# A two-layer decoder trunk on one core: 32x32 transposes on VectorE and DMAs between partition groups in place of TensorE transposes

## What is computed

```python
# layer one: stick-breaking attention
q, k, v, z = split(x @ w_in_a)                 # 2048 -> 4 x 2048
w = exp(log_sigmoid(s) + tail(log_sigmoid(-s)))  # s = q k^T / sqrt(128), past keys
y = ((w @ v) * silu(z)) @ w_out_a
# after each layer
x = layer_norm(2**0.5 * x + y)
x = x + (p[i] @ w_ple[i]) * sigmoid(x @ w_ple_gate[i])
# layer two: causal softmax attention against a shared, rotary K/V
k, v = split(layer_norm_kv(x) @ w_kv); k = rope(k)
q, z = split(x @ w_in_b);              q = rope(q)
y = ((softmax(q k^T / sqrt(128)) @ v) * silu(z)) @ w_out_b
```

## Time and profile before

| | |
|---|---|
| median of three runs | 1171.24 us |
| the profiled execution's own time | 1170.72 us |
| its span, first to last instruction | 1168.8 us |
| TensorE busy | 1161.9 us, 99% |
| VectorE busy | 740.9 us, 63% |
| ScalarE busy | 591.1 us, 51% |
| share of the 16 DMA engines, queue of SyncE | 57.7% |

### The profile page before, as it was taken

One profiled execution on the slowest core, in us unless ns is written; L12 is line 12 of the kernel. 1 busy time (PEld: TensorE's weight loads), 2 busy tenths in 40 slices (PEclk: granted clock), 3 DMA queues, 4 the chain that ended last, 5 costly groups with the idle time before them and its releaser, 6 DMA issues.

```text
span 1168.8 us, 15615 instructions
## 1 busy us (share of the span) xinstructions
PE 1161.9 (99%) x5484; PEld 971.4 (83%) x5484; DVE 740.9 (63%) x786; ACT 591.1 (51%) x669; POOL 21.3 (2%) x43
## 2 busy tenths in 40 slices
PE   9999999999999999999999999999999999999998
PEld 7888888888888888888888888888888888888886
DVE  6765556556556556688777665446677666656863
ACT  6665465456446543455444445544555545435541
POOL 1000000000000000000000000000000000000000
PEclk9999999999999999999999999999999999999999
DMA  9855656665565776457765655655545575763671
GB/s 307 287 161 178 181 162 178 179 181 161 165 194 156 241 253 200 137 184 237 232 198 162 197 180 182 193 181 164 169 155 178 167 244 175 252 195 112 211 252 41
DMA packets 112618, 221.49 MB, mean 189 GB/s; under 512 B 6929, under 2 KB 8977, under 8 KB 112065
## 3 DMA queue, kind: packets, MB, share of 16 engines
q1 hardware_dynamic: 110032, 209.74, 57.7%
q0 software_dynamic: 2544, 11.19, 2.7%
HBM read 216.71 MB, written 4.19 MB: 189 GB/s over the span
## 4 chain that ended last, share of the span: by engine, by line
PE 95%; DVE 2%; DMA 1%; ACT 1%; issue 0%; SPq 0%; ACTq 0%; DVEq 0%
PE acc L1077 29%; PE acc L1079 29%; PE acc L1078 29%; PE aux L1104 2%; PE aux L1121 2%; DVE w_lo L676 1%; PE aux L1145 1%; DVE stage L870 1%; PE aux L1159 1%; DMA raw<-in_w_ple_gate 1%; PE aux L1308 0%; DMA raw<-in_w_in_a 0%; DVE act L691 0%; PE aux L1079 0%; PE aux L1078 0%
## 5 line engine op out<-in xcount | busy, mean ns | idle before, releaser
L676 DVE TENSOR_TENSOR w_lo<-raw,w_hi 128x1024 fp32r<-128x1024 f32 x388 | 471.7, 1224 | 358.5 <-ACT w_hi L417 357.2
L417 ACT ACTIVATE w_hi<-raw 128x1024 fp32r<-128x1024 f32 x388 | 409.7, 1060 | 471.3 <-PE acc L1079 424.5
L1077 PE MATMUL acc<-w_hi,act 128*128 128x512 f32 x1552 | 611.9, 394 | 0.2 <-DVE w_lo L767 0.2
L1079 PE MATMUL acc<-w_hi,act 128*128 128x512 f32 x1552 | 605.1, 390 | 0.0
L1078 PE MATMUL acc<-w_lo,act 128*128 128x512 f32 x1552 | 604.1, 389 | 0.0
L1079 PEld LDWEIGHTS acc<-w_hi,act 128*128 128x128 f32 x1552 | 291.3, 188 | 61.8
L1077 PEld LDWEIGHTS acc<-w_hi,act 128*128 128x128 f32 x1552 | 291.5, 188 | 58.6 <-issue 1.0
L1078 PEld LDWEIGHTS acc<-w_lo,act 128*128 128x128 f32 x1552 | 291.7, 188 | 58.1
L430 ACT ACTIVATE act<-stage 128x1024 fp32r<-128x1024 f32 (+1 forms) x12 | 12.7, 1061 | 33.8 <-DVE stage L870 33.8
L513 ACT ACTIVATE heads<-aux,neg_max 128x128 f32<-128x128 f32 (+1 forms) x32 | 13.0, 419 | 23.7 <-DVE neg_max L1000 23.7
L691 DVE TENSOR_TENSOR act<-stage,act 128x1024 fp32r<-128x1024 f32 (+1 forms) x12 | 14.7, 1226 | 14.3 <-ACT act L430 14.3
(11 more groups left out here) (148 smaller groups left out, 617.5 us busy)
## 6 DMA issues: line engine op xcount, KB each, us to landing
raw<-in_w_in_a SPq DMA_DIRECT2D x124, 512.0 KB, 3.7
raw<-in_w_ple_gate SPq DMA_DIRECT2D x64, 512.0 KB, 4.8
raw<-in_w_in_b SPq DMA_DIRECT2D x64, 512.0 KB, 3.7
raw<-in_w_kv SPq DMA_DIRECT2D x64, 512.0 KB, 3.7
raw<-in_w_out_a SPq DMA_DIRECT2D x32, 512.0 KB, 4.4
raw<-in_w_out_b SPq DMA_DIRECT2D x32, 512.0 KB, 4.9
heads<-in_ln_rows POOLq DMA_DIRECT2D x4, 1024.0 KB, 8.2
raw<-in_w_ple SPq DMA_DIRECT2D x8, 512.0 KB, 4.6
```

Of the source, the lines that this page charges most:

```text
L417: nc.scalar.activation(w_hi[:, r], raw[:, r % RAWS], ACT.Copy).then_inc(hi_ready, 1)
L676: nc.vector.tensor_tensor(w_lo[:, r], raw[:, r % RAWS], w_hi[:, r].bitcast(F32), ALU.subtract) \
L1077: nc.tensor.matmul(dst, hi, w_hi[:, r, i], start=begin, stop=False)
L1079: mm = nc.tensor.matmul(dst, lo, w_hi[:, r, i], start=False, stop=end)
```

## The change

All transposes of q, k and z in layer one, of q and z in layer two, of the key/value operand and of three of four quarters of x2 leave TensorE. In their place:

- VectorE transposes 32x32 blocks (`turn_squares`, `turn_queries`, `turn_normed`, a step in `add_ple`), 128x1024 in one instruction. For q, k, z it takes the place of the copy out of `acc`.
- SyncE then moves the blocks between groups of 32 partitions: `exchange` issues 16 DMAs of 32 partitions x 256 values (32 KB each), in four batches of four, each batch after one of its loads. The batches stand after loads 3, 4, 5, 6 of a chunk (SOON), or eight after load 5 and eight after load 6 (LATE), or after 1 and 2 (MIDDLE).
- ScalarE and VectorE read the blocks through access patterns that put them in order, from SBUF instead of PSUM (`q_copies`, `k_copies`, `silu_z`, `x2_hi`, `ln_quarter`); `q_copies` copies all 256 tokens twice.
- The steps on the other engines move: `x2_hi` from after piece 3 to 6, `copy_qT` from 2 to 6, `silu_z` of layer two from 2 to 5. `k_copies` stays after piece 2 and `key_scores` after piece 4.
- The copy of x2 after its sum is gone.
- The last ple product of layer two (12 matmuls of 128x512) goes behind the last gate chunk, as 18 matmuls in three parts (`last_ple_product`), and the final product, sum and store are cut into three parts.

```diff
@@ SyncE @@
+            def exchange(turned, count, dst, src, moved, at):
+
+                def group(i):
+                    if i == 0:
+                        sp.wait_ge(turned, count)
+                    rows = slice(i * SQUARE, (i + 1) * SQUARE)
+                    for g in range(NS):
+                        sp.dma_start(dst[g * SQUARE:(g + 1) * SQUARE, i * HT // NS:(i + 1) * HT // NS],
+                                     src[rows, g * HT // NS:(g + 1) * HT // NS]).then_inc(moved, 16)
+
+                return {j: [lambda i=i: group(i) for i in range(NS) if at[i] == j] for j in at}
+
+            SOON, LATE, MIDDLE = (3, 4, 5, 6), (5, 5, 6, 6), (1, 1, 2, 2)
...
-                load_chunk(n, 0, wa, g + 2 * G)
-                load_chunk(n + PC, 0, wa, g + 3 * G)
+                load_chunk(n, 0, wa, g + 2 * G, q_exchange_a(g * 4))
+                load_chunk(n + PC, 0, wa, g + 3 * G, k_exchange_a(g * 4 + 1))
                 load_chunk(n + 2 * PC, 0, wa, g + 1)
-                load_chunk(n + 3 * PC, 0, wa, g + 1 + G)
+                load_chunk(n + 3 * PC, 0, wa, g + 1 + G, z_exchange_a(g * 4 + 3))
...
+            with sp.Fori(2, G + 2) as c:
+                load_chunk(c * PC + N_Q, N_Q, wb, c, ln_exchange(c - 2) | q_exchange(c - 2))
@@ ScalarE @@
             def k_copies(k):
 
-                act.wait_ge(kT_psum, k + 1)
-                nc.scalar.activation(kT[:, :, P:T], aux_kt[1][:, :, P:T], ACT.Copy).then_inc(kT_ready, 1)
-                nc.scalar.activation(k_parts[:, 0], aux_kt[1][:, :, 0:P], ACT.Copy).then_inc(k_hi, 1)
+                act.wait_ge(k_moved, k * MOVED + MOVED)
+                nc.scalar.activation(by_square(k_own), kT_x[:, 1::TT], ACT.Copy).then_inc(kT_ready, 1)
+                nc.scalar.activation(by_square(k_parts[:, 0]), kT_x[:, 0::TT], ACT.Copy).then_inc(k_hi, 1)
@@ VectorE @@
-            def evacuate(n_end, parity, dst):
+            def turn_squares(n_end, parity, dst):
+
                 dve.wait_ge(piece_used, n_end)
-                nc.vector.tensor_scalar(dst, acc_of(parity), 1.0, None, ALU.mult).then_inc(chunk_evac, 1)
+                nc.vector.transpose(turned_squares(dst), turned_rows(acc_of(parity))).then_inc(chunk_evac, 1)
...
+                nc.vector.tensor_tensor(r, r, stage_tn, ALU.add).then_inc(x2_ready, 1)
+                if layer == 0:
+                    dve.wait_ge(x2_ready, e + 1)
+                    if turn:
+                        nc.vector.transpose(turned_squares(vz_flat), turned_rows(r)).then_inc(x2_turned, 1)
+                    statistics(r, c)
@@ TensorE @@
             def after_v(k, c):
-                return {2: [lambda: k_turn(k, c - 1)], 4: [lambda: key_scores(k, 0)],
+                return {4: [lambda: key_scores(k, 0)],
                         5: [lambda: key_scores(k, 1)]}
...
-            with pe.Fori(1, G) as c:
-                chunk(c * PC + N_Q, N_Q, act1, c % 2, c + C_Q,
-                      after={2: [lambda: q_turn_b(c - 1)], 5: [lambda: ln_step(c)]})
-            chunk(N_Z, N_Z, act1, 0, C_Z, after={2: [lambda: q_turn_b(G - 1)]})
-            with pe.Fori(1, G) as c:
-                chunk(c * PC + N_Z, N_Z, act1, c % 2, c + C_Z, after={2: [lambda: z_turn_b(c - 1)]})
+            chunk(N_Q, N_Q, act1, 0, C_Q, quarters=S_X2, after={2: [last_x2_turn]})
+            with pe.Fori(1, 2 * G) as c:
+                chunk(c * PC + N_Q, N_Q, act1, c % 2, c + C_Q)
```

More of the change, by code:

```diff
@@ L926, in out_ple_gate @@
                           + [lambda r=r: normalise(r, r) for r in x1] + turned[0]})
-                pieces(N_PLE[layer], N_PLE[layer], count=G,
-                       before={0: turned[1], 2: turned[2]})
+                pieces(N_PLE[layer], N_PLE[layer], count=G - layer,
+                       before={0: turned[1], 2 - layer: turned[2]})
                 n = N_GATE[layer]
-                pieces(n, n, {4: [lambda: gain_and_offset(layer, 0)], PC - 1: [lambda: add_ple(layer, 0)]},
+                pieces(n, n, {4: [lambda: gain_and_offset(layer, 0)], PC - 1: [lambda: add_ple(layer, 0, layer == 0)]},
@@ L931, in out_ple_gate @@
                        before={0: turned[3]})
-                with dve.Fori(1, G - layer) as c:
-                    pieces(c * PC + n, n, ({3: [lambda: x2_lo(c - 1)]} if layer == 0 else {})
-                           | {5: [lambda: gain_and_offset(layer, c)], PC - 1: [lambda: add_ple(layer, c)]})
+                if layer == 0:
+                    for c in range(1, G):
+                        pieces(c * PC + n, n, {5: [lambda: gain_and_offset(0, c)], 6: [lambda: x2_lo(c - 1)],
+                                               PC - 1: [lambda: add_ple(0, c, c < G - 1)]})
+                else:
+                    with dve.Fori(1, G - 1) as c:
+                        pieces(c * PC + n, n, {5: [lambda: gain_and_offset(1, c)], PC - 1: [lambda: add_ple(1, c)]})
@@ L935, in out_ple_gate @@
                 if layer:
                     c = G - 1
+                    pieces(n + c * PC, n, count=1)
                     gain_and_offset(layer, c)
-                    dve.wait_ge(ple_evac, 2 * G)
                     dve.wait_ge(x1_ready, 2 * G)
-                    for t in range(TT):
-                        r, gate = columns(res[1], c)[:, t], stage_tn[:, t]
+                    for i, (t, lo, hi) in enumerate(LAST_PARTS):
+                        r, gate = columns(res[1], c)[:, t, lo:hi], stage_tn[:, t, lo:hi]
@@ L990, in k_end @@
+            pieces(N_Z, N_Z, {2: [lambda: ln_quarter(G - 1)], 3: [lambda: ln_lo(G - 1)]} | z_end(0, 0))
+            for c in range(1, G):
+                pieces(c * PC + N_Z, N_Z, z_end(c, c % 2))
             def k_end(n, g):
@@ L1194, in _ @@
             chunk(0, 0, act0, 0, 0, quarters=S_X)
-            chunk(PC, 0, act0, 1, 1, after=after_k(0, 1))
+            chunk(PC, 0, act0, 1, 1)
             pe.wait_ge(masks_done, 1)
@@ L1236, in ple_and_gate @@
                 pe.wait_ge(p_ready, layer + 1)
-                for c in range(G):
+                for c in range(G - layer):
                     n = N_PLE[layer] + c
@@ L1248, in ple_and_gate @@
                 chunk(n, n, act0, 0, c0, quarters=s, after={1: [lambda: turn(3)]})
[L1249 removed]
+                if layer == 0:
+                    pe.wait_ge(ple_evac, G)
                 with pe.Fori(1, G - layer) as c:
[L1251 to L1252 removed]
+                    chunk(c * PC + n, n, act0, c % 2, c + c0)
                 if layer:
```

338 lines of the change are left out of this document (198 added, 140 removed).

## The result

The changed kernel takes 1231.41 us, the median of four runs (1228.64 to 1232.58), against 1171.07 us for the kernel before on the same chip: a ratio of 1.0513, 95% interval 1.0494 to 1.0531. It is 5.1% slower. I had forecast 1166.5 us, a range of 1152 to 1175, and a chance of 0.14 for slower. Both sign and size were wrong. The profiled execution took 1228.64 us, its span is 1226.7 us.

The account below looks back on a forecast made before the run. TensorE, busy 99% of the span, was taken as the bound. From 1170.72 us: -23.9 transposes, +9.9 and +7.5 waits before the scores, +2.0 clock, +0.8 norm, -0.5 end = 1166.5 us, range 1152 to 1175.

Parts of the forecast that it names:

- the waits before the scores: Layer one, TensorE waiting for k: +7.5 us in the first head group and 3 x 3.3 = +9.9 us in the others.
- the low clock: TensorE's clock falls once, behind the 7.5 us wait, and stays low 4 us: +2.0 us, bounds 0 and 4.
- the norm: Layer two, gate product one ple piece earlier against the norm, so its operand comes late: +0.8 us, bounds 0 and 2.
- The end: After the last matmul: sigmoid and most products lie beside the last ple product, two half-width instructions follow: -0.5 us.
- step 2: SyncE issues k's four batches 0.47 us per DMA; load 6 waits for v's lo part, last DMA out at 161.05.
- Behind the wait nothing starves: Layer one, groups two to four: weight parts run eight pieces (21.8 us) ahead, so TensorE does not lack weights.
- the tightest place: SyncE in layer two's q chunks: 40 issues at 0.47 take 18.8 of 21.8 us; exchanges there cost nothing in the sum.
- 0 to 2 us is in the range: The x2 exchange makes the sigmoid up to 5 us later; x2's last transposes have about half a microsecond left.
- the row at the end: Profile row after the last matmul: clock falls some 4.8 us after TensorE stopped, so waits of 3.3 us were thought too short.
- Late landing: Rival: 32 KB DMAs of the k exchanges and first q exchange land 4.2 us after issue: 1183 us, chance 0.14.
- nothing much: Rival: small waits (first group 10, clock 4, x2 2) eat the advance: 1171 us, chance 0.14.
- the low bounds of the steps: Layer one, the path to k at its lowest step times: 1.3 us of wait a group said to remain.

Follow-up runs that it names:

- experiment 1: The changed kernel with each exchange as 4 DMAs of 128 partitions instead of 16, same bytes, movement between partition groups left out, result not valid: 1176.58 us.
- experiment 7: The changed kernel with 8 of the 16 DMAs of every exchange issued by GpSimd and 8 by SyncE: 1156.72 us, ratio 0.9876 to the kernel before.
- experiment 12: The kernel of experiment 7 unchanged, measured once more on the same chip: 1156.31 us, ratio 0.9865 to the kernel before.

## Why the prediction was wrong

Against the profiled execution, 1228.64 us, the forecast of 1166.5 lacks 62.1 us. By its terms: the waits before the scores were 41.3 us where the sum had 17.4 (23.9 too little); x2, the last z, the out projection and the weight parts waited 25.3 us, for which it had nothing; the low clock cost 15.5 us for 2.0; the norm cost nothing for 0.8.

**What held.** 104 of 320 transposes are left; with the account above, 0.887 us for a group of eight is right. The block transpose took 1.24 us for the 1.22 taken. The landing behind the last batch was 1.8 us for 2.1. The wait came where it was forecast, before the scores, released through `k_parts`, longest in the first group. The end gained 0.5 us: from the start of the last matmul to the end of the last sum it is 2.0 us (1222.30 to 1224.30) for 2.5. A fall of the clock costs 2.6 us where I had 2.0. And where the issues do not set the pace, the working of the path holds: in experiment 1 the last batch went out 9.3 us after the block transpose (9.9 in my steps), the scores of groups two to four wait 3.4 to 3.5 us for the 3.3 forecast, those of the first 6.7 for 7.5. That this agreement is so close is partly luck, as the 128 KB DMAs land later there than the 2.1 us that I took.

**The step that failed first is step 2, the issues.** I took 0.47 us from one issue to the next, out of two DMAs of 128 rows or more in the start-up, with 0.6 as the upper end; it is 0.61. And I wrote that "issue speed is not what counts in the end", since load 6 would wait for a weight part. At 0.47 a batch and a load take 2.35 us and fit into a piece of 2.72. At 0.61 they take 3.13 and do not. The error in one number was small; it moved the pace from the weight parts to SyncE. The last of the 16 went out 13.1 us after the block transpose began (166.85 to 179.95), where my working had 9.9. I kept 0.6 in the range, but never put it through the chain, where it does not cost 16 x 0.13 = 2 us but changes which thing waits for which.

**The second is the sentence "Behind the wait nothing starves".** I checked the lead of the weight parts only against TensorE's need of weights, and that was right (0.8 us of such waits). I did not ask what else stands in the list behind those parts: every step of VectorE and ScalarE, the block transpose among them. It made the second to fourth wait 3 us longer, and the first 14.0 instead of 7.5 us.

**Layer two and x2.** I had counted the exchanges there as free and named the tightest place: 40 issues on SyncE in a q chunk, 24.0 of 21.8 us at 0.6, "up to 2.2 us for each of four chunks". The 8.8 us of four such chunks are near the 9.0 measured, but they came in one piece at the last z, four z chunks later and behind that z's own exchange, so the agreement may be chance. I had left them out of the sum, since my 0.47 stood. For x2, "0 to 2 us is in the range"; it was 11.6. As I read the rows, eight issues before load 6 and eight before load 7 hold the loads back, so ScalarE comes late to `x2_hi` and the sigmoid. That fits the runs with fewer issues on SyncE, 0.5 us in experiment 1, 4.2 and 2.7 in experiments 7 and 12, but no run takes it apart further.

**The clock.** One fall, I said, behind the wait of 7.5 us, as the row at the end has the full clock for four microseconds after the last matmul. In experiment 1 the windows behind waits of 3.4 and 3.5 us show 0.50 (171.00 to 173.00, 270.40 to 272.40), in experiment 7 behind 3.2 us as well (66.80 to 69.00). In experiment 12 it is at 0.50 behind 2.7 us (590.70 to 593.00) and at 1.00 behind 2.1 us (66.00 to 72.00). The row at the end does not say what a wait in the middle does. This step alone, the clock at 9.5 us in experiment 1 where the sum has 2.0, would have taken the gain from 4.2 us to nothing even with the issues as cheap as I thought.

The Trainium skill (TensorE: Matmul & The Clock Gate, Why this matters for your kernels; I had named the section wrongly) asks for no idle gaps between bursts of matmuls. The falls behind all the waits of the change bear it out: strictly read it was worth 6 us in my sum, and it was the better guide.

**The norm** costs nothing, where I had 0.8.

**The rivals.** "Late landing" was the one of the right sign, with the wrong cause: landing had a median of 2.9 us for `heads<-big` and 2.5 to 2.8 for the others, just the 2.9 from which I said the gain would be gone. But experiment 7 has landings of 3.3 (SyncE) and 2.7 us (GpSimd) for `heads<-big`, on SyncE 3.1 to 4.3 us for the others, and is faster. I had held issue cost and landing to be one case; they are not, for issues add up on a queue (0.61 us each) and landings overlap. Two slips in the working of the rivals change none of this: the terms of "nothing much" add up to 1173, not 1171 us, and at the low bounds of the steps a group would still wait 2.2, not 1.3 us.

The Trainium skill's rule on merging (DMA: Bandwidth & Descriptors, Rules for kernel authors), that transfers under 64 KB are mostly overhead, pointed at this: experiment 1 puts the price of the 12 issues more per exchange, with the movement between groups, at 55 us. Whether the blocks can move between the groups in fewer DMAs no run tried. The Trainium skill's rule that leaves a 128x128 transpose to TensorE (VectorE: DVE Perf Modes, Rules for kernel authors) held for the change as it stands, but not by VectorE, whose block transpose took what its copy took, and not once the issues are on two queues: experiment 7 beats TensorE's transposes.

## What to carry to other kernels

When DMAs are put into a queue that paces something else, add up all issues of a period by the time that such a DMA takes to issue, and compare with the period at the upper end of that time too; past the period the queue becomes the pace, and its lateness goes to everything behind it. A lead that covers the consumer does not cover the steps that other engines hang on the same list: ask what stands behind each late item. And before giving up such a change, look for an idle engine that can issue: half of the DMAs on a second queue turned 5% slower into 1% faster.

## What the runs showed of the hardware

- A DMA of 32 partitions x 256 values between SBUF places is issued in 0.59 us on SyncE (0.61 from start to start), a weight load of 512 KB in 0.38 to 0.59; on GpSimd such a small DMA takes 0.50 us, less than the 0.72 of one of its 512 KB loads. I had expected the small one on SyncE to be no dearer than a large one, and GpSimd to be the slower of the two.
- SyncE's and GpSimd's issues run side by side (experiment 7: 152.66 to 158.26 and 152.92 to 157.00). Landings on SyncE are then longer: 3.3 us for `heads<-big` where one queue had 2.9, 3.8 and 3.9 for `heads<-stage` and `heads<-heads` (2.8), 4.3 for `stage<-v_or_z` (2.5); on GpSimd they are 2.1 to 3.7.
- VectorE's block transpose of 128x1024 float32 values out of PSUM takes 1.24 us, as its copy does (1.22).
- TensorE's clock was at 0.50 after waits of 3.2 and of 2.7 us in the middle of dense work, at 1.00 after one of 2.1 us, and came back within about five microseconds; one such fall cost 2.6 us in the second group of the change.
